# Feed-forward in-products: one 512-column matmul over x's high and low part, plus one of 256 columns, in place of three of 256

## The reference

```
def rms_norm(x, gain):
    y = xf * lax.rsqrt(jnp.mean(xf * xf, axis=-1, keepdims=True) + EPS)
    return (y * gain).astype(x.dtype)
def swiglu_ffn(h, w_in, w_out):
    gate, up = jnp.split(h @ w_in, 2, axis=-1)      # 1024 -> 2 x 2816
    return (jax.nn.silu(gate) * up) @ w_out          # 2816 -> 1024
x = x + FFN_RESID * swiglu_ffn(rms_norm(x, ffn1_norm[l]), ffn1_w_in[l], ffn1_w_out[l])
```

## Time and profile before

| | |
|---|---|
| median of 3 runs | 1847.29 us |
| profiled execution: its time, its span | 1848.8 us, 1847.1 us |
| matmuls busy | 1809.4 us, 98% of the span |
| DVE busy, ACT busy | 1017.4 us (55%), 791.3 us (43%) |
| granted TensorE clock, mean | 0.99 |

### The profile page before, as it was taken

The page is one execution under the profiler, slowest core; times in us unless marked ns, Lnnn a source line. Parts: engine busy times, 40 slices in busy tenths (PEclk is TensorE's granted clock), DMA queues, the critical chain, the costliest instruction groups (busy, mean ns, idle before and its releaser), DMA issues.

```text
span 1847.1 us, 26827 instructions
## 1 busy us (share of the span) xinstructions
PE 1809.4 (98%) x11336; PEld 1581.2 (86%) x11336; DVE 1017.4 (55%) x1208; ACT 791.3 (43%) x863; POOL 77.6 (4%) x145
## 2 busy tenths in 40 slices
PE   8999999999999999999999999999999999999998
PEld 8998797877999899987978779998878964869996
DVE  4555366986654455453669775455775422235553
ACT  4554355543654355443554535553303111135542
POOL 0000000000000000000000001000751000000000
PEclk9999999999999999999999999999997999999999
DMA  7537254444654545561544448664343224236471
GB/s 251 182 126 277 80 176 153 156 137 141 224 181 182 205 145 183 186 237 51 189 160 144 153 160 165 210 222 168 115 136 69 81 68 156 94 102 219 134 273 57
DMA packets 194331, 293.13 MB, mean 159 GB/s; under 512 B 9298, under 2 KB 128884, under 8 KB 194244
## 3 DMA queue, kind: packets, MB, share of 16 engines
q1 hardware_dynamic: 191988, 287.72, 46.0%
q0 software_dynamic: 1936, 4.14, 2.1%
q10 hardware_dynamic: 320, 0.01, 0.0%
HBM read 289.49 MB, written 2.36 MB: 158 GB/s over the span
## 4 chain that ended last, share of the span: by engine, by line
PE 91%; DVE 3%; ACT 3%; DMA 2%; issue 1%; ACTq 0%; DVEq 0%; SPq 0%
PE acc L225 21%; PE acc L227 21%; PE acc L226 21%; PE acc L271 4%; PE acc L194 3%; PE acc L206 3%; PE acc L2616 2%; PE acc L2924 1%; DMA ring<-in_ffn_w_in 1%; PE acc L457 1%; PE acc L253 1%; PE acc L1297 1%; ACT big L1425 1%; PE acc L2319 1%; PE turn L338 1%
## 5 line engine op out<-in xcount | busy, mean ns | idle before, releaser
L425 DVE TENSOR_TENSOR w_lo<-ring,w_hi 128x2048 fp32r<-128x2048 f32 x160 | 361.7, 2290 | 211.5 <-ACT w_hi L421 211.5
L225 PE MATMUL acc<-xT_hi,w_hi 128*128 128x256 f32 x1680 | 476.4, 284 | 1.7 <-DVE w_lo L425 1.3
L226 PE MATMUL acc<-xT_lo,w_hi 128*128 128x256 f32 x1680 | 475.8, 283 | 0.0
L227 PE MATMUL acc<-xT_hi,w_lo 128*128 128x256 f32 x1680 | 475.8, 283 | 0.0
L421 ACT ACTIVATE w_hi<-ring 128x2048 fp32r<-128x2048 f32 x160 | 301.1, 1911 | 150.3 <-PE acc L227 100.1
L225 PEld LDWEIGHTS acc<-xT_hi,w_hi 128*128 128x128 f32 x1680 | 322.7, 192 | 2.3 <-DVE w_lo L425 1.5
L226 PEld LDWEIGHTS acc<-xT_lo,w_hi 128*128 128x128 f32 x1680 | 322.7, 192 | 0.0
L227 PEld LDWEIGHTS acc<-xT_hi,w_lo 128*128 128x128 f32 x1680 | 322.7, 192 | 0.0
L225 PE MATMUL acc<-w_hi,hT_hi 128*128 128x512 f32 x440 | 172.4, 392 | 0.0
L227 PE MATMUL acc<-w_hi,hT_lo 128*128 128x512 f32 x440 | 171.4, 390 | 0.0
L226 PE MATMUL acc<-w_lo,hT_hi 128*128 128x512 f32 x440 | 171.4, 390 | 0.0
(11 more groups left out here) (531 smaller groups left out, 2850.6 us busy)
## 6 DMA issues: line engine op xcount, KB each, us to landing
ring<-in_ffn_w_in SPq DMA_DIRECT2D x88, 1024.0 KB, 5.9
ring<-in_w_in SPq DMA_DIRECT2D x52, 1024.0 KB, 5.1
ring<-in_ffn_w_out SPq DMA_DIRECT2D x44, 1024.0 KB, 6.0
ring<-in_w_branch SPq DMA_DIRECT2D x12, 1024.0 KB, 5.0
ring<-in_w_out SPq DMA_DIRECT2D x12, 1024.0 KB, 5.0
ring<-in_w_gate SPq DMA_DIRECT2D x11, 1024.0 KB, 5.2
ring<-in_w_up SPq DMA_DIRECT2D x11, 1024.0 KB, 7.0
ring<-in_w_down SPq DMA_DIRECT2D x11, 1024.0 KB, 6.0
```

What stands on the lines that cost most here:

```text
L225: pe.matmul(o, a_hi, wh, start=start, stop=False)
L226: pe.matmul(o, a_hi, wl, start=False, stop=False)
L227: return pe.matmul(o, a_lo, wh, start=False, stop=stop)
L425: vec.tensor_tensor(w_part(w_lo, r), raw_part(c0, r), w_part(w_hi, r).bitcast(F32), ALU.subtract).then_inc(f.lo, 1)
```

## The change

Per slice of 128 inputs the stationary w_hi meets x_hi and x_lo side by side in one matmul of 512 columns, and w_lo meets x_hi in one of 256, which is added to the first half. A tile of 128 features now fills a whole bank: columns 0 to 255 hold all but the x_lo part, 256 to 511 the x_lo part. So a block takes four banks: gate tiles in one pair, up tiles in the other, and each pair is used again in every block. The halves must be summed: ACT copies the second halves to SBUF (`rest`, two copies of 256 per half-block), DVE adds the first halves (`gate_sum`; in `hidden` for up). Silu now follows the sum, and the multiply too; both work in SBUF. The loop covers blocks 2 to 9, and blocks 0 and 1 are written out ahead of it. `products_done` is raised per half-block. x's parts lie interleaved in `x_parts`. The semaphores are shared by all feed-forwards, with offsets in place of a set for each. The number of groups, and what follows from it, is adapted.

```diff
@@ ffn_pe
-                for ft in range(2 * halves[0], 4):
-                    half, fs = ft // 2, slice(ft * P, (ft + 1) * P)
-                    if ft % 2 == 0:
-                        pe.wait_ge(f.lo, RING + 2 * jj + 1 + half + RING * i)
-                        wait_acc_free(pe, G, half, i)
-                    for k in range(KD):
-                        ins = three(pe, acc[bank(G, half)][:, (ft % 2) * TOK:(ft % 2 + 1) * TOK], wh[:, k, fs], wl[:, k, fs],
-                                    xT_hi[:, k, :], xT_lo[:, k, :], k == 0, k == KD - 1)
-                ins.then_inc(products_done, 2 if len(halves) == 2 else 1)
+                for half in halves:
+                    G = G0 + 2 * jj + half
+                    pe.wait_ge(f.lo, f.w0 + RING + 2 * jj + 1 + half + RING * i)
+                    for ft in range(2):
+                        fs = slice((2 * half + ft) * P, (2 * half + ft + 1) * P)
+                        wait_acc_free(pe, G, ft, 2 * i)
+                        o = acc[bank(G, ft)]
+                        for k in range(KD):
+                            pe.matmul(o[:, :], wh[:, k, fs], x_parts[:, k, :], start=(k == 0), stop=False)
+                            ins = pe.matmul(o[:, 0:TOK], wl[:, k, fs], xT_hi[:, k, :], start=False, stop=(k == KD - 1))
+                    ins.then_inc(products_done, 1)
@@ ffn_act
+            def rest(dst, r, G, i, used):
+                wait_products(act, c0 + r, i)
+                if used:
+                    wait_acc_read(act, G - 2, 1, 2 * i)
+                for ft in range(2):
+                    ins = act.activation(dst[:, ft, :], acc[bank(G, ft)][:, TOK:2 * TOK], ACT.Copy)
+                ins.then_inc(f.rest, 1)
+            def silu(jj, i):
+                for ft in range(2):
+                    wait_acc_read(act, G0 + 2 * jj, ft, 2 * i)
+                act.activation(gate_s[:, jj % 2], gate_s[:, jj % 2], ACT.Silu)
+            def copy_hT(jj, i):
+                act.wait_ge(f.h, f.h0 + jj + 1 + 2 * i)
+                act.activation(hT_hi[:, bass.ds(2 * jj + 4 * i, 2), :], h_s[:, jj % 2], ACT.Copy).then_inc(f.hT, 1)
+            def half_blocks(jj, i, r_gate, r_up, i_next, first=False):
+                split_act(act, f, c0, r_gate, i_next)
+                if first:
+                    first_silu()
+                else:
+                    rest(gate_rest, 2 * jj, G0 + 2 * jj, i, True)
+                    silu(jj, i)
+                split_act(act, f, c0, r_up, i_next)
+                rest(up_rest, 2 * jj + 1, G0 + 2 * jj + 1, i, not first)
+                copy_hT(jj, i)
+            half_blocks(0, 0, 2, 3, 0, first=True)
+            half_blocks(1, 0, 4, 5, 0)
+            with act.Fori(1, PAIRS) as i:
+                half_blocks(0, i, 2, 3, i)
+                half_blocks(1, i, 4, 5, i)
+            half_blocks(NFB - 1, 0, N_IN, N_IN + 1, 0)
@@ ffn_vec
+            def gate_sum(jj, i):
+                G = G0 + 2 * jj
+                vec.wait_ge(f.rest, f.r0 + 2 * jj + 4 * i)
+                for ft in range(2):
+                    vec.tensor_tensor(gate_s[:, jj % 2, ft, :], acc[bank(G, ft)][:, 0:TOK], gate_rest[:, ft, :],
+                                      ALU.add).then_inc(acc_read[bank(G, ft)], 1)
+            def hidden(jj, i):
+                G = G0 + 2 * jj + 1
+                vec.wait_ge(f.rest, f.r0 + 2 * jj + 1 + 4 * i)
+                for ft in range(2):
+                    vec.tensor_tensor(h_s[:, jj % 2, ft, :], acc[bank(G, ft)][:, 0:TOK], up_rest[:, ft, :],
+                                      ALU.add).then_inc(acc_read[bank(G, ft)], 1)
+                for ft in range(2):
+                    wait_acc_read(vec, G, ft, 2 * i)
+                vec.tensor_tensor(h_s[:, jj % 2], h_s[:, jj % 2], gate_s[:, jj % 2], ALU.mult).then_inc(f.h, 1)
+            def half_blocks(jj, i, r_gate, r_up, i_next, first=False):
+                split_vec(vec, f, c0, r_gate, i_next)
+                if not first:
+                    gate_sum(jj, i)
+                split_vec(vec, f, c0, r_up, i_next)
+                hidden(jj, i)
+                rest_hT(jj, i)
```

More of the change, by code:

```diff
@@ L456, in first_gate @@
                                 pe.wait_ge(n.vec, n.turned(2 * m + k // 4))
-                            ins = pe.matmul(acc[bank(G0, 0)][:, ft * TOK + m * P:ft * TOK + (m + 1) * P],
+                            ins = pe.matmul(acc[bank(G0, ft)][:, m * P:(m + 1) * P],
                                             raw_part(c0, 0)[:, k, ft * P:(ft + 1) * P], xT[:, k, m * P:(m + 1) * P],
@@ L508, in ffn_act @@
         def ffn_act(act, f, c0, G0, asides={}):
[L509 to L519, removed]
-                act.activation(hT_hi[:, bass.ds(2 * jj + 4 * i, 2), :], h_s[:, jj % 2], ACT.Copy).then_inc(f.hT, 1)
@@ new lines, in first_silu @@
+            def first_silu():
+                wait_products(act, c0)
+                for ft in range(2):
+                    act.activation(gate_s[:, 0, ft, :], acc[bank(G0, ft)][:, 0:TOK], ACT.Silu).then_inc(acc_read[bank(G0, ft)], 1)
+            def silu(jj, i):
[4 more added lines that the diff above has]
+                act.wait_ge(f.h, f.h0 + jj + 1 + 2 * i)
+                act.activation(hT_hi[:, bass.ds(2 * jj + 4 * i, 2), :], h_s[:, jj % 2], ACT.Copy).then_inc(f.hT, 1)
@@ L541, in split, with rest_hT @@
                 split_vec(vec, f, c0, 2 * jj + 1, i)
[L543 to L549, removed]
+            def gate_sum(jj, i):
[7 more added lines that the diff above has]
+                vec.wait_ge(f.rest, f.r0 + 2 * jj + 1 + 4 * i)
+                for ft in range(2):
+                    vec.tensor_tensor(h_s[:, jj % 2, ft, :], acc[bank(G, ft)][:, 0:TOK], up_rest[:, ft, :],
+                                      ALU.add).then_inc(acc_read[bank(G, ft)], 1)
+                for ft in range(2):
+                    wait_acc_read(vec, G, ft, 2 * i)
+                vec.tensor_tensor(h_s[:, jj % 2], h_s[:, jj % 2], gate_s[:, jj % 2], ALU.mult).then_inc(f.h, 1)
+            def rest_hT(jj, i):
+                vec.wait_ge(f.hT, f.h0 + jj + 1 + 2 * i)
                 part = bass.ds(2 * jj + 4 * i, 2)
@@ L552, in rest_hT @@
                                   hT_hi[:, part, :].bitcast(F32), ALU.subtract).then_inc(f.hT_lo, 1)
[L554 to L564, removed]
+            def half_blocks(jj, i, r_gate, r_up, i_next, first=False):
[5 more added lines that the diff above has]
+                rest_hT(jj, i)
+            half_blocks(0, 0, 2, 3, 0, first=True)
+            half_blocks(1, 0, 4, 5, 0)
+            with vec.Fori(1, PAIRS) as i:
+                half_blocks(0, i, 2, 3, i)
+                half_blocks(1, i, 4, 5, i)
+            half_blocks(NFB - 1, 0, N_IN, N_IN + 1, 0)
             for r in range(N_IN + 2, N_IN + KF // 2):
@@ L1582, in merged_in_act @@
                     act.wait_ge(mt.vec, 1 + b)
-                    act.activation(quarter(xT_hi, b), quarter(xT, b), ACT.Copy).then_inc(tail.act, 1)
+                    act.activation(quarter(merged_hi, b), quarter(xT, b), ACT.Copy).then_inc(tail.act, 1)
             def merged_in_vec(vec, m):
@@ L1938, in params2_pool @@
         def params2_pool(pool, before):
-            pool.wait_ge(before, 8)
+            pool.wait_ge(before.hi, before.w0 + 8)
             for name, r in (("s5_a_re_2", "are"), ("s5_a_im_2", "aim")):
```

70 lines of the change are left out of this document (39 added, 31 removed).

## The result

The changed kernel takes 1884.16 us (median of 4 runs, 1883.77 to 1884.9) against 1848.15 (4 runs): ratio 1.0188, 95% interval 1.0169 to 1.0207, so slower by 1.9%. The forecast was 1873 in a range of 1852 to 1903. The profiled execution has a span of 1882.7, which is 35.6 more than before; 25.8 had been forecast.

What follows compares the result with a forecast made beforehand. TensorE bound the kernel before; afterwards the alternating ACT and DVE chain would. The profiled span of 1847.1 plus 19.4 (five feed-forwards) plus 6.4 (late load) gives 1872.9; the median 1847.3 plus 25.8 gives 1873.1, predicted 1873, range 1852 to 1903.

Steps and rivals of the forecast that it cites:

- TensorE's pair, 0.3464: In-products: one 512-column matmul (0.2264 us) plus one of 256 (0.120) replace three (0.360); 22.8 us less if TensorE stays bound.
- The cycle, 11.88: Feed-forward loop: alternating ACT and DVE steps add up to 11.88 us per block, above TensorE's new 11.08 and the old 11.52.
- TensorE's waits in the loop: Sign for the forecast: in the loop PE idles once or twice a block, some 0.8 us in all.
- PE busy below 96% in these stretches: Sign for the forecast: PE's busy share in the stretches of the feed-forward loop falls below 96%.
- no wait of PE between half-blocks: Sign against the forecast: in the loop, PE goes from one half-block to the next without waiting.
- A feed-forward, +3.9: Block 0's up product to down's fourth matmul: 125.0 us instead of 121.2, so 3.9 longer; five feed-forwards give 19.4.
- the out-products keep their time: Out-products after the loop: no change in time, a chunk of 24 matmuls taking 5.43 us.
- The late load, +6.4: Layer 1's second feed-forward: a ring load delayed by POOL's parameter loads stalls the chain 7.9 us, 6.4 more than before.
- The table loads: Rival: ACT table loads stay in the loop, one on the chain per pass; 28.6 us more, 1902 us; chance 0.25.
- TensorE stays the bound: Rival: the ACT and DVE cycle hides under TensorE's 11.08 us block; 22.8 less, 2.9 back, 1827 us; chance 0.09.

Runs made afterwards that it cites:

- the first experiment: The changed kernel with a block's Silu on ACT moved behind the split of the next up chunk; 1843.4 us, ratio 0.9957 to the kernel before.
- both splits first: The changed kernel with both splits of the next block ahead of the gate's sum and Silu, on ACT and DVE; 1848.84 us, ratio 0.9981 to the kernel before.
- the grouped kernel: The changed kernel with Silu behind the up split and, per feature tile, eight 512-column matmuls, then eight of 256; 1836.81 us, ratio 0.9923 to the kernel before.
- the run with the shorter filler: The changed kernel with 10 spare float32 matmuls of 256 columns ahead of each feed-forward's fourth out-product; 1875.81 us, ratio 1.0131 to the kernel before.

## Why the prediction was right, and where its sizes were off

*TensorE's pair, 0.3464.* Off by a little. PE's timeline in the changed kernel:
```profile
67.94 0.40 PE L452 MATMUL acc<-x_parts,w_hi 128*128 128x512 f32 x1
68.18 0.28 PE L453 MATMUL acc<-x_parts,w_lo 128*128 128x256 f32 x1
68.29 0.40 PE L452 MATMUL acc<-x_parts,w_hi 128*128 128x512 f32 x1
...
70.06 0.40 PE L452 MATMUL acc<-x_parts,w_hi 128*128 128x512 f32 x1
```
Six pairs in 70.06 - 67.94 = 2.12 us are 0.353 each. Of the 0.0136 to be gained 0.007 is left, and a block takes TensorE 11.30, not 11.08. But this is not a fixed price. PE's timeline in the fifth feed-forward of the first experiment, the same program at clock 1.00:
```profile
1700.20 0.39 PE L452 MATMUL acc<-x_parts,w_hi 128*128 128x512 f32 x1
...
1702.28 0.39 PE L452 MATMUL acc<-x_parts,w_hi 128*128 128x512 f32 x1
```
Six pairs in 2.08 us are 0.347 each, what the forecast said, and all of that feed-forward's pairs have this mean (0.3467); its in-products take 2.3 us less than those of the first three (0.3533). With both splits first, three of the five feed-forwards have 0.3467. So the alternation of widths doesn't cost the 0.007 by itself, and a comparison with the grouped kernel's 0.349 depends on which feed-forward is taken; what decides between the two prices stays open. In the changed kernel the price made no difference, since the chain was behind: its second feed-forward has pairs of 0.348 in the mean and takes 125.69 us from block 0's up product to the fourth out-product, the first has 0.353 and takes 125.78. The Trainium skill ("TensorE: Matmul & The Clock Gate", "Back-to-back issue gap") gives columns / 2.4 GHz + 2.5 ns as the gap of an isolated matmul and says that in a stream of weight loads and matmuls both set the spacing; the formula would make the pair 0.325, an estimate, and no feed-forward here comes below 0.3467.

*The cycle, 11.88.* Right: 11.90 in the loop, 11.78 in the blocks ahead of it. Every rung is there, and the adds, which no row of before showed, last 0.416 (L576) and 0.417 (L583). No rung is off by more than 0.06, so the sum is not right by luck. That the edge through Silu makes it was shown by taking it out (11.31, TensorE's own) and by lengthening it (12.14 and 12.23).

*TensorE's waits in the loop, "once or twice a block, some 0.8 us in all", "PE busy below 96% in these stretches".* These signs did not come, and "no wait of PE between half-blocks", which was to show the forecast wrong, is what most of the loop has: PE is busy for 112.48 of 113.00 us and the pairs run on from one half-block to the next. The forecast had TensorE pay for the slower chain in each block. The runs showed that it starts the loop with its splits 4 us ahead and pays once, at the fourth out-product. The working for a whole feed-forward goes by the chain's end and so is not touched by this.

*A feed-forward, +3.9.* The mechanism and the moment were right: the fourth out-product was put 125.7 us behind the start of block 0's up product, 25.09 + 125.7 = 150.8, and it is at 150.87. The size of the step after it was not: the working said "the out-products keep their time". They take 63.42 from the fourth on, where they took 60.92, since the wait of 4.50 us that the same working implied is followed by half the clock. That is 2.5 us in this feed-forward and 11.4 in all five, more than the whole miss of 9.8; the run with the shorter filler took it away. The fault was to put TensorE's idle time down as waiting only, and not to ask at what clock it goes on.

*The late load, +6.4.* Right in kind, 1.7 us too much. Timeline of ACT, second feed-forward of layer 1, after:
```profile
1186.84 1.91 ACT L430 ACTIVATE w_hi<-ring 128x2048 fp32r<-128x2048 f32 x1 [6.18 <-DMA ring<-in_ffn_w_in]
```
ACT waits 6.18 us, with no lead left to absorb it, where 7.9 was forecast. From block 0's up product to the fourth out-product this feed-forward takes 132.05 us and the others 125.76 in the mean; before it was 123.43 and 121.89. So the load costs 6.3 in place of 1.5, 4.75 more. Together: 25.8 forecast, + 11.4 for the clock, - 1.7 for the load, + 0.1 in small changes of both signs, is the 35.6 measured. The two misses have opposite signs; that the sum is off by 9.8 and not by 11.4 is luck.

*The table loads.* The rival is false. The group in the changed kernel:
```profile
L533 ACT ACT_TABLE_LOAD x5 | 6.4, 1283 | 0.1
```
Five, one at each feed-forward's first Silu, none in the loop. Entering the loop with Silu's table present was enough, as the rows behind the loop had suggested. It would have cost 28.6.

*TensorE stays the bound.* False here, and true once Silu stands behind the split. The rival put the gain at 22.8 less 2.9; with pairs of 0.353 there are 11.8 to win (1680 x 0.007), and the kernel without the edge is 6.9 faster than the kernel before beside it.

## What to carry to other kernels

When work goes from one engine to two that run queues in order, write both queues as one ladder and add up the steps from one block to the next: an alternation of two engines at 42% and 58% can be the bound, and moving one waiting instruction (Silu) behind one that is ready (the split) took 41 us off. Don't look for its cost in the loop alone: an engine with a lead stays 99.5% busy there and pays at the next place that needs the chain's last result. Price a matmul by its distance to the next one, not by its duration, and over several stages: the same pairs cost 0.3467 us in one feed-forward and 0.3533 in another. And where a forecast leaves TensorE waiting for some us in one piece, add what the lower clock costs afterwards.

## What the runs showed of the hardware

- An idle time of 4.50 us on TensorE was followed by 5.4 us at half the clock, 2.50 us lost; the same place with filler had clock 1.00. It is not always as much: of the five such places the fourth lost 1.35. Waits of 0.5 us (the first experiment) cost nothing of the kind. The Trainium skill ("TensorE: Matmul & The Clock Gate", "What's actually happening") describes a clock that falls to 1.2 GHz when the engine idles; the trace agrees.
- Matmuls in flight all the time do not protect the clock. In the first state mixer of the changed kernel it fell in the middle of such a stretch, behind matmuls of 8 columns. The same place after and before, and a later place of the same mixer before:
```profile
234.00:238.00 4.00, 4.00 (x13) 3.09 (x12) 4.00 (x5) 1.49 (x1) 0.00 (x0) 0.60 0.00 1
```
```profile
228.00:232.00 4.00, 4.00 (x19) 3.26 (x18) 4.00 (x5) 1.50 (x1) 0.00 (x0) 1.00 0.00 0
...
410.00:414.00 4.00, 4.00 (x14) 3.33 (x14) 4.00 (x5) 0.00 (x0) 0.00 (x0) 0.57 0.01 5
```
  Before the change the mixer had its lower clock at 410 us, behind matmuls of 128 columns and a wait of 2.1 us; hence the mixers' equal times. The kernel with 10 spare matmuls had both. Each costs some 1.6 us. What decides between them was not settled.
- A 512-column matmul and a 256-column one that alternate stand some 0.235 and 0.117 apart, 0.353 together, in most feed-forwards, and 0.347 together in others of the same execution; grouped by eight they take 0.349.
- An fp32 matmul of 256 columns is recorded as two passes and takes 0.43 us, where an fp32r one takes 0.12.
